# Stick-breaking sums on VectorE, and another order and other PSUM banks at the last v tile and the first and last experts, in a hybrid attention and mixture-of-experts block

## The reference, cut to what matters

```python
h = rmsnorm(x)
fq, fk, fv, f_logit, sq, sk, sv = split(h @ w_in)          # FoX and stick-breaking q, k, v
# stick-breaking, for each block of 128 queries and the keys before it:
z = q @ k.T * scale
log_1mb = where(strict, log_sigmoid(-z), 0)
suffix = cumsum(log_1mb, reverse=True) - log_1mb           # sum over all later keys
a = exp(where(strict, log_sigmoid(z) + suffix, -inf))      # then a @ v
# FoX: softmax(q @ k.T * scale + c_query - c_key) @ v, c the running sum of log forget gates
x = x + concat(rmsnorm(fox), rmsnorm(stick)) @ w_out
# top 4 of 32 experts of each token, rows gathered by expert:
act = min(glu, 7) * sigmoid(1.702 * glu) * (clip(lin, -7, 7) + 1)   # glu, lin: halves of x @ w1 + b1
x = x + sum over experts of weight * (act @ w2 + b2)
y = rmsnorm(x)
```

## Time and profile before

| | |
|---|---|
| time, median of 3 runs | 1519.27 us (1519.02 to 1520.36) |
| time of the profiled execution | 1524.51 us |
| its span, first to last instruction | 1522.7 us |
| mean granted TensorE clock | 0.984 |
| PE busy | 1476.2 us (97%) |
| PE weight loads busy | 1195.4 us (79%) |
| DVE busy | 1333.1 us (88%) |
| ACT busy | 1103.4 us (72%) |
| POOL busy | 264.2 us (17%) |
| HBM traffic over the span | 307 GB/s |

### The profile page before, as it was taken

How to read it: one execution, slowest core, us unless ns; L and a number is a source line. 1 busy time by engine, 2 the same in 40 slices (tenths; PEclk the granted TensorE clock), 3 DMA queues, 4 the chain that set the end, 5 groups by cost and what they waited for, 6 DMA issues and landing times.

```text
span 1522.7 us, 22431 instructions
## 1 busy us (share of the span) xinstructions
PE 1476.2 (97%) x7111; PEld 1195.4 (79%) x7111; DVE 1333.1 (88%) x1520; ACT 1103.4 (72%) x1313; POOL 264.2 (17%) x202
## 2 busy tenths in 40 slices
PE   7999999998999999999999999999999999999995
PEld 5788787786888888888888877888888888888874
DVE  5576665569899999999999999999999999999986
ACT  5566554355788888888878888888888888788774
POOL 5000000037022211111121111222111111211110
PEclk9999998989999999999999999999999999999997
DMA  8021021269999999999999999999999999999943
GB/s 248 16 83 56 29 83 56 68 235 378 371 372 369 379 353 377 375 366 367 380 363 371 368 367 372 356 380 373 359 364 371 377 370 362 372 369 367 360 166 120
DMA packets 100216, 451.84 MB, mean 297 GB/s; under 512 B 13458, under 2 KB 25746, under 8 KB 67408
## 3 DMA queue, kind: packets, MB, share of 16 engines
q1 hardware_dynamic: 90848, 434.68, 75.0%
q0 software_dynamic: 9328, 16.64, 4.6%
HBM read 445.18 MB, written 22.54 MB: 307 GB/s over the span
## 4 chain that ended last, share of the span: by engine, by line
PE 71%; DVE 18%; issue 7%; ACT 4%; POOL 0%; DVEq 0%; ACTq 0%; POOLq 0%
PE zpair L2078 42%; DVE stage_lo L1160 8%; PE bank L2078 7%; PE bank L1701 4%; PE bank L1702 3%; PE bank L1703 3%; DVE qk L1575 3%; ACT stage_hi L779 2%; DVE act_lo L1547 2%; DVE qk L1571 2%; PE bank L2045 2%; PE zpair L1785 1%; PE bank L1849 1%; PE bank L1800 1%; PE zpair L2056 1%
## 5 line engine op out<-in xcount | busy, mean ns | idle before, releaser
L1160 DVE TENSOR_TENSOR stage_lo<-ring,stage_hi 128x1024 fp32r<-128x1024 f32 x796 | 954.7, 1226 | 43.8 <-ACT stage_hi L779 7.9
L779 ACT CAST stage_hi<-ring 128x1024 fp32r<-128x1024 f32 x796 | 828.2, 1054 | 195.5 <-PE zpair L2078 153.7
L2078 PE MATMUL zpair<-stage_hi,act_hi 128*128 128x512 f32 x1024 | 324.1, 398 | 2.3 <-DVE stage_lo L1160 2.3
L2078 PE MATMUL zpair<-stage_lo,act_hi 128*128 128x512 f32 x1024 | 316.9, 391 | 0.0
L2078 PE MATMUL zpair<-stage_hi,act_lo 128*128 128x512 f32 x1024 | 316.5, 390 | 0.0
L2078 PEld LDWEIGHTS zpair<-stage_lo,act_hi 128*128 128x128 f32 x1024 | 192.8, 188 | 41.2
L2078 PEld LDWEIGHTS zpair<-stage_hi,act_lo 128*128 128x128 f32 x1024 | 192.7, 188 | 40.9
L2078 PEld LDWEIGHTS zpair<-stage_hi,act_hi 128*128 128x128 f32 x1024 | 187.2, 188 | 47.4 <-DVE stage_lo L1160 11.9
L665 POOL COPY sidx<-gtab 128x1 int32 (+1 forms) x31 | 109.3, 3526 | 391.7 <-ACT qk L1060 391.7
L2078 PE MATMUL bank<-stage_hi,act_hi 128*128 128x512 f32 x512 | 164.6, 403 | 6.9 <-DVE stage_lo L1160 4.3
L2078 PE MATMUL bank<-stage_lo,act_hi 128*128 128x512 f32 x512 | 159.1, 392 | 0.0
(11 more groups left out here) (317 smaller groups left out, 1479.5 us busy)
## 6 DMA issues: line engine op xcount, KB each, us to landing
ring<-in_w SPq DMA_DIRECT2D x384, 1024.0 KB, 7.5
ring<-in_w_in SPq DMA_DIRECT2D x12, 1024.0 KB, 5.3
ring<-in_w_out SPq DMA_DIRECT2D x4, 1024.0 KB, 4.9
xs_all<-in_x SPq DMA_DIRECT2D x4, 512.0 KB, 7.8
ring<-in_x SPq DMA_DIRECT2D x4, 512.0 KB, 3.8
tn_scratch<-qk SPq DMA_DIRECT2D x4, 512.0 KB, 3.5
x_scratch<-ring SPq DMA_DIRECT2D x4, 512.0 KB
ring<-x_scratch SPq DMA_DIRECT2D x4, 512.0 KB, 5.2
```

The costliest lines, as they stand in the source:

```text
L779: nc.scalar.copy(dst, src).then_inc(split_hi, 1)
L1160: nc.vector.tensor_tensor(dst, src, hi_ap.bitcast(F32), ALU.subtract).then_inc(split_lo, 1)
L2078: mm = pe.matmul(bank[b0 + h][:], w[:, k, :], m[:, j % STAGES, h * BANK:(h + 1) * BANK], start=start and w is T_hi and m is stage_hi, stop ...
```

## The change

**Stick steps.** The scores are made with queries on the partitions. The two sets of PE products with triangular and all-ones matrices go, with their constants. DVE makes the sums with one scan along the keys, backward, for each head (`log_weights`), and subtracts from z. The weights are then not turned: PE turns them (`turn_stick`), the first block of a pair into its z bank, the other three into banks 6 and 7; ACT and DVE copy them to the buffers `pt_hi` and `pt_lo` which FoX uses too (`stick_turned`, `stick_rest`), early, a step or two behind; one `pv_stick` of 24 matmuls for each pair replaces four of 6.

**Last v tile.** `LAST_V` is step 27. ACT copies `v_hi` of tile 23 before that step's `fox_exp`, DVE makes `v_lo` before `fox_scale`; before, both stood behind them and behind `pt_hi` and `pt_lo` of the step before.

**First two experts.** The glu half of expert 0 goes to banks 4 and 5. Expert 1's rows are turned after piece 12 of expert 0, and the first half of them is copied before the second expert's body. Expert 1's biases open banks 0 and 1 at once, and banks 2 and 3 after its first piece. DVE clips lin after the first and glu after the third piece of the body, and ACT's gate of expert 0 waits for both. Row and weight tables move to banks 0 and 1 and the filler matmuls to bank 5.

**Last expert.** Its activations are turned before the last w2 piece of the expert before, copied in halves between the first pieces of its own w2, and its result goes to banks 0 and 1 in place of 4 and 5, so that `y_evac` of the expert before moves behind three more pieces. `onehot` and the reading of `n_over` stand before `last_low`; `FIN` is the order of the banks of the last sums.

```diff
-FIN = (0, 2, 6, 4)
+FIN = (4, 2, 6, 0)
...
@@ scalar @@
+                nc.scalar.activation(pbuf[:, s % 2, :, 0:n], lbuf[:, s % 2, :, 0:n], ACT.Exp).then_inc(a_ready, 1)
+            def stick_turned(s):
+                i = s % TT
+                act.wait_ge(st_turned, s + 1)
...
+                for m in range(2):
+                    ins = nc.scalar.copy(pt_hi[:, m, i:4 * i + 1:3, :], turned_at(s, m)[:, 0:(i + 1) * P].rearrange("p (k q) -> p k q", q=P))
+                ins.then_inc(st_hi_r, 1)
...
+                if 2 <= s < STICK + 2 and (s - 2) % TT:
+                    stick_turned(s - 2)
                 if s < STICK:
                     softplus_tail(s)
                 elif s < STEPS:
+                    if s == LAST_V:
+                        v_evac(2 * PAIRS - 1)
                     fox_exp(s)
                 if 1 <= s <= STICK:
                     stick_exp(s - 1)
+                    if s % TT == 1:
+                        stick_turned(s - 1)
...
-                act.wait_ge(clipped, 2 * t + 1)
+                act.wait_ge(clipped, 2 if isinstance(t, int) and t == 0 else 2 * t + 1)
...
-                y_evac(q0 + n - 2, ub + 24 * n - 8)
-                a_evac(q0 + n - 1)
                 for j in range(W2P):
                     hi_moe(j, z, turns(z, T0 + c // SLOTS + 1), ub + 24 * n - 8 + j - STAGES + 1)
+                    if j == 1:
+                        a_evac(q0 + n - 1, (0,))
+                    if j == 2:
+                        act.wait_ge(used, ub + 24 * n - 8)
+                        a_evac(q0 + n - 1, (1,))
+                    if j == 3:
+                        y_evac(q0 + n - 2, ub + 24 * n - 8)
@@ vector @@
-            def softplus(s):
-            def stick_split(s):
+            def log_weights(s):
+                n, l = (s % TT + 1) * P, lbuf[:, s % 2]
+                dve.wait_ge(ln_ready, s + 1)
+                chained(nc.vector.scalar_tensor_tensor(out=l[:, :, 0:n], in0=zpair[s % 2][:, :, 0:n], scalar=0.0,
+                                                       in1=l[:, :, 0:n], op0=ALU.max, op1=ALU.add))
+                for m in range(2):
+                    back = l[:, m, 0:n][:, ::-1]
+                    loose(nc.vector.tensor_tensor_scan(back, back, ones[:, 0:1].to_broadcast([P, n]), 0.0, ALU.add, ALU.mult))
+                dve.wait_ge(steps["dve"], count["dve"])
+                nc.vector.tensor_tensor(l[:, :, 0:n], zpair[s % 2][:, :, 0:n], l[:, :, 0:n], ALU.subtract).then_inc(loga_ready, 1)
+            def stick_rest(s):
+                dve.wait_ge(st_hi_r, s + 1)
...
                 if s < STICK:
                     lower((s, True))
-                    softplus(s)
+                    if s >= 2 and s % TT != 2:
+                        stick_rest(s - 2)
+                    log_weights(s)
+                    if s % TT == 1:
+                        stick_rest(s - 1)
...
                     added_early(s)
+                    if s == LAST_V:
+                        proj_lo_part(TILES - 1)
                     fox_scale(s)
...
                         lo_moe(j, (j // 2 + 8) % SLOTS, run.split(r, j))
+                        if j == 1 and first and b == MOE0:
+                            clip_first(1)
+                        if j == 2 and first and b == MOE0:
+                            clip_first(0)
+                            turned_lo(xT_lo, xT_hi, xT_hi_r, xT_lo_r, q0 + 1, (1,))
...
+            dve.wait_ge(last_col, 1)
+            row_marks()
+            n_over = dve.value_load(novi[0:1, 0:1], min_val=0, max_val=OVER)
             last_low()
@@ tensor @@
-            def log_a(s):
+            def turn_stick(s):
+                c, i = divmod(s, TT)
+                pe.wait_ge(a_ready, s + 1)
+                if i == 1:
+                    wait(pe, mix_lo, 2 * c)
+                elif i:
+                    pe.wait_ge(st_lo_r, s)
...
+            def pv_stick(c):
+                pe.wait_ge(st_lo_r, TT * (c + 1))
+                pe.wait_ge(proj_lo, 3 * c + 3)
+                weigh(c).then_inc(pvs_done, TT)
...
-                    if part == 1 and 1 <= s <= STICK:
-                        log_a(s - 1)
+                    if part == 1 and s % TT == 1 and TT < s < STICK + TT:
+                        pv_stick(s // TT - 1)
+                    if part == (1 if s > TT else 2) and s % TT == 1 and s < STICK:
+                        turn_stick(s - 1)
-                    if part == 2 and 2 <= s < STICK + 2:
-                        pv_stick(s - 2)
...
+                if 1 <= s <= STICK and s % TT != 1:
+                    turn_stick(s - 1)
...
-                    multiply(j, run.split0 + j + 1, xT_hi, xT_lo, j // 2, 2 * (j % 2), j >= W1P - 2)
-                turn_x(q0 + 1)
+                    multiply(j, run.split0 + j + 1, xT_hi, xT_lo, j // 2, 2 if j % 2 else 4 if b == MOE0 else 0, j >= W1P - 2)
+                    if j == 12 and b == MOE0:
+                        turn_x(q0 + 1)
...
+                        if last and j == 6:
+                            turn_a(t)
...
-                turn_a(q0 + n - 1)
-                pe.wait_ge(aT_lo_r, 2 * (q0 + n))
-                second_free(q0 + n - 1)
+                pe.wait_ge(aT_lo_r, 2 * (q0 + n) - 1)
+                if b == MOE0:
+                    pe.wait_ge(clipped, 2 * n)
```

More of the change, by code:

```diff
@@ L940, in evacuate @@
                         proj_evac(tile)
-                    if tile % 3 == 2 and place(turn_part(tile)) == at:
+                    if tile % 3 == 2 and tile < TILES - 1 and place(turn_part(tile)) == at:
                         v_evac(tile // 3)
@@ L1258, in fox_max @@
+            def stick_rest(s):
+                i = s % TT
+                dve.wait_ge(st_hi_r, s + 1)
+                for m in range(2):
+                    ins = nc.vector.tensor_tensor(pt_lo[:, m, i:4 * i + 1:3, :], turned_at(s, m)[:, 0:(i + 1) * P].rearrange("p (k q) -> p k q", q=P),
+                                                  pt_hi[:, m, i:4 * i + 1:3, :].bitcast(F32), ALU.subtract)
+                ins.then_inc(st_lo_r, 1)
             def fox_max(s):
@@ L1342, in lower @@
                     if tile % 3 == 2:
-                        if place(turn_part(tile)) == at:
+                        if tile < TILES - 1 and place(turn_part(tile)) == at:
                             proj_lo_part(tile)
@@ L1563, in weights, with clip_first @@
                 nc.vector.tensor_copy(wcol[:], at_col(wtab, i)).then_inc(weight_ready, 1)
+            def clip_first(part_):
+                if part_:
+                    dve.wait_ge(used, MAIN.base - OPROJ_PIECES + W1P)
+                    for h in range(2):
+                        ins = nc.vector.tensor_scalar(lin[:, h * BANK:(h + 1) * BANK], bank[2 + h][:], LIMIT, -LIMIT,
+                                                      ALU.min, ALU.max)
+                else:
+                    for h in range(2):
+                        ins = nc.vector.tensor_scalar(glu[:, h * BANK:(h + 1) * BANK], bank[4 + h][:], LIMIT, None, ALU.min)
+                ins.then_inc(clipped, 1)
             def clip(t, part_, used_at):
@@ L1775, in z_scores @@
                 mm.then_inc(scored, 1)
-            def log_a(s):
-                i, zb = s % TT, bank[2 * (s % 2):2 * (s % 2) + 2]
-                pe.wait_ge(sp_ready, s + 1)
-                for v in range(i + 1):
-                    o, w = P * v * (v + 1) // 2, P * (v + 1)
-                    for m in range(2):
-                        for part in (sp_hi, sp_lo):
-                            mm = pe.matmul(zb[m][:, (i + 1) * P - w:(i + 1) * P], (neg_tri if v == i else neg_one)[:], part[:, m, o:o + w],
-                                           start=False, stop=v == i and part is sp_lo, skip_group_check=True)
-                mm.then_inc(loga_ready, 1)
@@ L1789, in pv_stick @@
-            def pv_stick(s):
-                p, i = divmod(s, TT)
-                j, n, b = TT - 1 - i, (i + 1) * P, s % 2
-                pe.wait_ge(av_lo_r, s + 1)
-                if i == 0:
-                    pe.wait_ge(proj_lo, 3 * p + 3)
-                    if p:
-                        pe.wait_ge(mix_lo, 2 * p)
-                for m in range(2):
-                    for w, x in ((v_hi, av_hi), (v_hi, av_lo), (v_lo, av_hi)):
-                        mm = pe.matmul(obank[m][:, j * P:S], w[:, p % 2, j, :], x[:, b, m, 0:n],
-                                       start=i == 0 and w is v_hi and x is av_hi, stop=i == TT - 1 and w is v_lo, skip_group_check=True)
-                mm.then_inc(pvs_done, 1)
+            def turn_stick(s):
[5 more added lines that the diff above has]
+                    pe.wait_ge(st_lo_r, s)
+                for m in range(2):
+                    for kb in range(i + 1):
+                        mm = pe.transpose(turned_at(s, m)[:, kb * P:(kb + 1) * P], pbuf[:, s % 2, m, kb * P:(kb + 1) * P], identF[:])
+                mm.then_inc(st_turned, 1)
@@ new lines, in weigh @@
+            def weigh(ph):
```

(21 more changed lines are left out.)

189 lines of the change are left out of this document (99 added, 90 removed).

## The result

The kernel after takes 1502.92 us (median of 4 runs, 1500.37 to 1504.46), the kernel before 1519.46: a ratio of 0.9882 (0.9861 to 0.9904). Timed again on another chip it was 0.9880 (0.9863 to 0.9898). By the ratio that is 18 us less (the two medians lie 16.5 apart), where 22.6 were forecast; the time lies in the range of 1485 to 1509, 6.2 us above the number. The profiled execution fell by 20.05 us, from 1524.51 to 1504.46, its span by 20.0.

What follows compares the result with a forecast made beforehand. PE was taken to set the time nearly everywhere, with three stops over 3 us. Terms of -6.5, -6.3, -2 and -7.8 sum to -22.6 us, from 1519.3 to 1496.7 us; range 1485 to 1509, its own forecast 1491 to 1502.

Steps and rivals of the forecast that it cites:

- Stick steps: Four pairs of stick-breaking heads: PE sheds 13.2 us, half given back to late copies, -6.5 us; bounds -13.2 and +13.
- Last v: Last v tile: the 3.29 us stop and half clock go, a 1.35 us stop comes, -6.3 us.
- at 1.2 GHz PE spent 9.4 us: Behind the last v's stop: 4.7 us would be saved at full clock if all scaled; 4.4 taken.
- Experts 0 and 1: Passage between the first two experts: PE starts expert 1 earlier but stops before piece 3, -2 us; bounds -5 and +2.2.
- Last expert and end: Last w2 pieces and final sums and norms: the last norm ends at 1511.8 against 1519.65, -7.8 us.
- They land in time: At the end: loads of x behind the last scatter start near 1495.2 and land near 1498 to 1502, in time.
- The loop: Experts 2 to 30: not touched by the change, so no gain or loss was counted.
- DVE the bound: Rival: DVE, busy 25.9 of 27.7 us, bounds the stick steps, which give nothing: 1503 us; chance 0.18.
- All of PE's saving: Rival: PE's whole 13.2 us saving in the stick steps shows, total 1487 us; chance 0.12.
- Loads bound the experts: Rival: loads bound the experts and only the end keeps its gain, 1511 us; chance 0.04.
- Slower: Rival: a stop before `pv_stick` drops the clock in each pair, 1523.2 us; chance 0.04.
- the rule on transposes: Stick steps: by the skill's rule transposes don't keep the full clock; 20 more a pair would lower it somewhere in each.

Runs made afterwards that it cites:

- stick_only: The kernel before with only the stick-breaking steps changed: 1512.77 us, ratio 0.9937.
- half_scan: The kernel after with the running sum of each pair's second head left out: stick steps 152.82 against 155.42 us; whole 2074.53 us, as other weights change the routing.
- late_first_turn: The kernel after with the first step's turned copy and rest of pairs 1 to 3 moved behind their step's other work on ACT and DVE: 1508.16 us, 0.9910.
- fill_more: The kernel after with 14 more dummy matmuls in front of the transposes of expert 0's rows: 1501.84 us, ratio 0.9862.
- best: The kernel after with 14 more dummy matmuls before expert 0's rows and the first three output tiles' second biases ahead of the branch: 1502.33 us, 0.9873.
- no_v: The kernel after with only the order around the last v put back as before: 1507.73 us, ratio 0.9905.
- v_only: The kernel before with only the order around the last v changed: 1516.18 us, ratio 0.9954.
- after_timed: The kernel after, unchanged, timed again in the same call as later runs: 1503.67 us, ratio 0.9880.
- end_only: The kernel before with only the last expert and the end changed: 1515.10 us, ratio 0.9958.
- after_again: The kernel after, unchanged, profiled a second time: 1505.53 us profiled.

## Why the prediction was right, and where its sizes were off

The sign and the places were right, and so were the gains of the stick steps and of the last expert up to its last product. Last v and the passage from expert 0 to 1 were each 1 to 2 us too large, and another 1 us was lost in the loop, which I had put at nothing. Part of the agreement is luck. The measured 1502.9 us lies in the stated range, but just above the 1491 to 1502 us that I gave my own forecast, and it equals the 1503 of the rival by which the stick steps give nothing; the time alone can't tell the two apart. The table and stick_only do. In the following the means of its columns (two traces of before, three of after) stand against the terms; for the last v all traces with the same code there are taken.

**Stick steps: forecast -6.5.** It came as -7.2 in the passage. The scan's price held (1.21 us). The saving on PE was 11.4 us, not 13.2; the groups of products at 4.04 instead of 3.75 us are 1.2 of the difference. Given back are 4.2 us, not the half of 13.2 (4 x 1.65, which is 6.6 and not 6.5): before the groups PE stands 0.1 to 0.7 us rather than 0.9. The wait of 1.26 us for the exponential of the second pair's second step was foreseen in kind ("another 0.7 us"). That DVE holds some steps is shown by half_scan. The +0.7 us of start in the three traces after is no part of the term; half_scan too shows that one slower instruction of the norm, late_first_turn, fill_more and best don't.

**Last v: forecast -6.3.** The stop of 1.35 us before the scores of step 28 came as 1.21. The step that was mis-sized is "at 1.2 GHz PE spent 9.4 us, ... I take 4.4": that was one execution's luck. Stop and clock are worth 34.9 - 30.4 = 4.5 us over six and seven traces, 4.1 in time (no_v). What v_only has beyond it is not explained by this term.

**Experts 0 and 1: forecast -2.** The passage alone is right, 20.51 to 18.63 us, with the stop before piece 3 at 2.14 us (2.9 forecast). What I left out is the entry to expert 0. In the trace after the 22 filler matmuls ahead of the gathered rows run at full clock (2.58 us, 4.19 before), PE is then early, stands 1.66 us for the gather and is at half clock behind it; in after_timed it doesn't stand there and is at half clock ahead of it (4.11 us). PE waits or runs slowly. Routing and entry together are 144.75 us before and 143.8 after, -0.9, with 13.7 us of half clock between 300 and 350 on average in both.

**Last expert and end: forecast -7.8.** The first part of it is right: from the turn of the last expert's rows to its last product it is 64.73 us in the first trace before and 59.72 in the first after, -5.0 (5.2 forecast). The tail goes from 22.8 to 20.7 us, -2.1 (2.6 forecast), and end_only measures 6.4 for the whole. Two things in it are less sure than I wrote. "They land in time" is near its limit: one load is 0.36 us late in the trace after, and in best a load sets the first add. And the 3.01 us that DVE stands before `onehot`, which I took as given, were 0.71 in stick_only: over all traces with the same code there, five with the old end and seven with the new, the tail goes from 21.96 to 20.64 us, -1.3 only. With the new end it is 19.7 to 20.5 us where PE stands 2.3 to 2.7 us before the biases, and over 22 where it stands 3.7 or 3.9 and then runs them at half clock (late_first_turn, after_again).

**The loop: forecast 0.** Its 28 periods up to the turn of the last expert's rows take 994.7 us before and 995.1 to 996.2 in the three traces after, +1.0 on average, spread over all of them (35.51 to 35.55 us each before, 35.51 to 35.61 after). In best it is 994.9. The cause is open.

**Sum.** 0.7 - 7.2 - 4.5 - 0.9 - 5.0 + 1.0 - 2.1 = -18.0 us, against 18 by the ratio. And the step "the median is 5.2 us under the profiled one; I take the difference from it" kept the whole half clock of one profile as a gain: 4.4 us counted at the last v where six traces give 2.4 on average, 2 of the 4.6 us by which the sum missed.

**Rivals.** *DVE the bound*: excluded by stick_only. *All of PE's saving*: excluded by the time of stick_only; PE's stops and half_scan show what is given back. *Loads bound the experts*: the early experts' term is there, and the period of 35.5 us hasn't changed by 0.1; only at the very end are loads close to being the bound. *Slower*: the clock was 1.00 over all stick steps in the trace after. So the rule on transposes that was weighed ahead doesn't show itself in groups of 2 to 8 that stand between products.

## What to carry to other kernels

Before a profile's half clock is counted as a gain, profile the same kernel again: a stop of the same length cost 2.1 us in one run and 6.4 in another. Where several parts are to be added, cut both traces at the same instructions and compare the passages; the time of a part alone also carries what happened at places that it doesn't touch, here up to 4.1 us in a tail. ACT's waits of 4 us were free in the two pairs where they got shorter, and the edit that did it cost 3.1 us, because what was moved came to stand behind other work in DVE's queue.

## What the runs showed of the hardware

The clock of TensorE after a stop was not a function of the stop's length: 3.29 us were followed by 1.00 in one trace and by 0.50 over 9.4 us in another, at the same instruction; and in the trace after it fell around a stop of only 1.66 us, at 331.69. Windows of after:

```profile
327.00:330.00 3.00, 2.94 (x26) 2.50 (x24) 2.79 (x8) 0.00 (x0) 1.84 (x5) 1.00 0.37 108
330.00:333.00 3.00, 1.34 (x8) 1.34 (x8) 2.75 (x3) 0.19 (x1) 0.00 (x0) 0.65 0.21 85
333.00:336.00 3.00, 3.00 (x16) 2.25 (x16) 2.41 (x3) 1.07 (x3) 1.46 (x3) 0.50 1.13 229
```

A running sum backward takes 411, 678, 944 and 1211 ns for 128, 256, 384 and 512 columns, which is 2.08 ns for each further column. Forward it takes 1216 at 512. A subtraction of 512 columns takes 683 ns and one of 256 takes 415, 1.05 ns for each further column. "DVE: opcode table, instruction layouts, handler registers and perf-mode slots" of the Trainium skill says in its section 6, "Datapath and trigger behaviour", that this scan runs at half throughput; the rows agree (2.08 against 1.05 ns).
